# Attention of a decoder step on one Trainium2 core: four looped turns with pages loaded by half, against one written-out plan with 17 page places handed out in the order of use

## What is computed

```python
def diff_attention(q, k, v, q_pos, k_pos, rel_bias, lam, subln_g, lam_init):
    ...
    s = jnp.where(mask, s + bias, -jnp.inf)
    p = jax.nn.softmax(s, axis=-1)
    w = p[:, 0] - lam * p[:, 1]
    o = jnp.einsum('bhqk,bkhe->bqhe', w, v.astype(jnp.float32))
    o = o * lax.rsqrt(jnp.mean(o * o, axis=-1, keepdims=True) + SUBLN_EPS)
    ...
def stick_breaking_attention(q, k, v, q_pos, k_pos):
    ...
    log_rest = jnp.where(mask, jax.nn.log_sigmoid(-z), 0.0)
    suffix = lax.cumsum(log_rest, axis=3, reverse=True) - log_rest
    a = jnp.where(mask, jnp.exp(log_beta + suffix), 0.0)
    o = jnp.einsum('bhqk,bkhd->bqhd', a, v.astype(jnp.float32))
```

## Time and profile before

| | us |
|---|---|
| median of 3 runs | 1790.29 (1786.23 to 1792.81) |
| the profiled execution's own time | 1786.58 |
| its span, first to last instruction | 1784.7 |
| TensorE busy (matmuls) | 1381.3 (77%) |
| VectorE busy | 818.6 (46%) |
| ScalarE busy | 726.3 (41%) |
| DMA engines busy, mean share | 52% (q1 45.2%, q0 4.1%, q10 3.0%) |
| granted TensorE clock, mean | 0.890 |

### The profile page before, as it was taken

One profiled execution on the slowest core, in us unless ns is written; L12 is line 12 of the kernel. 1 busy time (PEld: TensorE's weight loads), 2 busy tenths in 40 slices (PEclk: granted clock), 3 DMA queues, 4 the chain that ended last, 5 costly groups with the idle time before them and its releaser, 6 DMA issues. The chain is left out here.

```text
span 1784.7 us, 30335 instructions
## 1 busy us (share of the span) xinstructions
PE 1381.3 (77%) x8924; PEld 1028.4 (58%) x8924; DVE 818.6 (46%) x1129; ACT 726.3 (41%) x1109; POOL 267.0 (15%) x200
## 2 busy tenths in 40 slices
PE   7999999967878787587878786688834888989930
PEld 4777778744545555354545453577623776777730
DVE  7021111125454545275757476322254555667635
ACT  5122221215454545353535354211104666677721
POOL 1000000000000000000000000000003455556644
PEclk9999999979898998798989998788856999999975
DMA  5333223146667666466666665432206799652248
GB/s 182 93 118 122 83 57 120 59 146 206 218 215 228 213 232 216 165 205 217 212 217 213 219 212 203 150 122 94 94 23 235 279 354 349 237 188 103 107 158 313
DMA packets 166779, 320.28 MB, mean 179 GB/s; under 512 B 20455, under 2 KB 59914, under 8 KB 162570
## 3 DMA queue, kind: packets, MB, share of 16 engines
q1 hardware_dynamic: 152666, 271.89, 45.2%
q0 software_dynamic: 7200, 26.22, 4.1%
q10 hardware_dynamic: 6800, 20.98, 3.0%
HBM read 313.33 MB, written 56.56 MB: 207 GB/s over the span
## 5 line engine op out<-in xcount | busy, mean ns | idle before, releaser
L1920 PE MATMUL gate_up_ps<-w_gate_up_split,slot_rows_T 128*128 128x512 f32 x768 | 196.3, 414 | 31.8 <-DVE slot_rows_T L1972 31.7
L1964 DVE TENSOR_TENSOR w_gate_up_split<-w_gate_up,w_gate_up_split 128x2048 fp32r<-128x2048 f32 x64 | 143.8, 2288 | 133.4 <-ACT w_gate_up_split L2018 133.4
L1888 POOL TENSOR_TENSOR w_down_split<-w_down,w_down_split 128x2048 fp32r<-128x2048 f32 x32 | 170.4, 5325 | 163.7 <-ACT w_down_split L2026 163.7
L874 PE MATMUL turns_and_scores_ps<-ident,pages 128*128 128x128 f32 (+1 forms) x1088 | 151.9, 286 | 53.1 <-DMA pages<-in_cache_s 31.4
L1920 PEld LDWEIGHTS gate_up_ps<-w_gate_up_split,slot_rows_T 128*128 128x128 f32 x768 | 150.5, 199 | 70.9 <-DVE slot_rows_T L1972 38.7
L255 PE MATMUL proj_ps<-w_in_hi,h_T_hi 128*128 128x512 f32 x432 | 174.4, 404 | 9.4 <-DVE w_in_lo L305 9.4
L874 PEld LDWEIGHTS turns_and_scores_ps<-ident,pages 128*128 128x128 f32 (+1 forms) x1088 | 125.0, 149 | 96.7 <-issue 95.8
L255 PE MATMUL proj_ps<-w_in_hi,h_T_lo 128*128 128x512 f32 x432 | 171.3, 396 | 0.0
L255 PE MATMUL proj_ps<-w_in_lo,h_T_hi 128*128 128x512 f32 x432 | 171.2, 396 | 0.0
L2018 ACT ACTIVATE w_gate_up_split<-w_gate_up 128x2048 fp32r x64 | 119.1, 1909 | 121.4 <-DMA w_gate_up<-in_w_up 86.6
L350 ACT ACTIVATE proj_rows<-proj_ps,sum_squares 128x512 f32<-128x512 f32 x54 | 37.1, 689 | 277.3 <-PE proj_ps L255 260.2
(11 more groups left out here) (220 smaller groups left out, 2150.5 us busy)
## 6 DMA issues: line engine op xcount, KB each, us to landing
pages<-in_cache_d SPq DMA_DIRECT2D x256, 256.0 KB, 3.1
pages<-in_cache_s SPq DMA_DIRECT2D x256, 256.0 KB, 3.1
w_gate_up<-in_w_gate SPq DMA_DIRECT2D x32, 1024.0 KB
w_gate_up<-in_w_up SPq DMA_DIRECT2D x32, 1024.0 KB
w_down<-in_w_down SPq DMA_DIRECT2D x32, 1024.0 KB
scratch_moe_out<-expert_out ACTq DMA_DIRECT2D x32, 512.0 KB
w_in_now<-in_w_in SPq DMA_DIRECT2D x48, 256.0 KB, 5.2
x_tiles<-in_x SPq DMA_DIRECT2D x9, 512.0 KB, 7.7
```

Of the source, the lines that this page charges most:

```text
L874: last = pe.transpose(kT_ps[:, KIND_BLOCKS * e + b, 0:n], page_rows[0:n, p, e, b, :], t.ident[0:n, 0:n])
L1888: pool.tensor_tensor(dn_split[:, u, 1, :, :], w_dn[:, bass.ds(at, 1), :, :].rearrange("p a k n -> p (a k) n"), dn_split[:, u, 0, :, :].bit ...
L1920: last = pe.matmul(gu_ps[:, u, :], xT[:, u, a, k, :], gu_split[:, u, b, k, :], start=(k == 0 and m == 0), stop=(k == KC - 1 and m == 2))
L1964: dve.tensor_tensor(gu_split[:, u, 1, at, :].rearrange("p k (c n) -> p k c n", c=2), raw[:, at, :, :], gu_split[:, u, 0, at, :].bitcast(F3 ...
```

## The change

The loops over turns go: the list of steps now covers all four turns, each engine walks it once, and every step carries its turn `it`. `prompt_steps` runs on from the last tile of a turn to the first of the next. Keys of turn it+1 are used between the values of turn it. Pages have 17 places (`PAGE_PLACES`) that keys and values take in the order of use: SP loads the first 17 uses, and after each use loads the use that is 17 further on. q, k, v, near (DIFF) and oT have two buffers each. Page scores take places in the ring (57 uses per turn in DIFF, 53 in STICK), and the sample output keeps a bank alone. The store of oT goes from ScalarE to SP. In DIFF the reciprocal of the sample sums goes from `weigh` to `rows`; in STICK the product of the sample weights is made in two parts, pages 0 to 7 first.

```diff
-SPANS = {DIFF: ((0.02, 0.45), (0.45, 0.53), (0.56, 1.0)), STICK: ((0.02, 0.45), (0.45, 0.53), (0.56, 1.0))}
+N_WEIGH = {DIFF: 2, STICK: 3}
+PAGE_PLACES = 17
+FIRST_KEYS, LAG, END_KEYS = 0.30, 0.02, 0.31
+WEIGH_AT, USE_AT, END_USE = 0.34, 0.42, 0.30
...
+    tiles = [(it, i) for it in range(TURNS) for i in range(PT)]
+    out = scores(0, 0) + scores(0, 1) + soft(0, 0, 0) + soft(0, 0, 1) + soft(0, 0, 2)
+    for n, (it, i) in enumerate(tiles):
+        one = tiles[n + 1] if n + 1 < len(tiles) else None
+        two = tiles[n + 2] if n + 2 < len(tiles) else None
+        out += soft(*one, 0) if one else []
...
+        if i == 1 and it:
+            out.append((("store", it - 1), 0))
...
+    for it in range(TURNS):
...
+        use = [(("turn", it, g), 1) for g in range(V_GROUPS)]
+        use += [(("apply", it, p), 2) for p in range(D_PAGES)] + [(("rows", it), 1), (("heads", it), 1)]
+        step = (TURNS - END_USE) / TURNS
+        begin = it * step
+        timed += spread_over(pages, 0 if it == 0 else begin - step + USE_AT + LAG, FIRST_KEYS if it == 0 else begin + END_KEYS)
+        timed += spread_over([(("weigh", it, n), 1) for n in range(N_WEIGH[kind])], begin + WEIGH_AT, begin + USE_AT - 0.02)
+        timed += spread_over(use, begin + USE_AT, begin + step + END_USE)
+    timed.sort(key=lambda x: x[0])
...
-        if name not in ("score", "page", "turn", "turn_out") and not (
+        if name not in ("score", "page", "page_scores", "turn", "turn_out") and not (
...
-        page_rows = sb("pages", [P, D_PAGES, PAIR, KIND_BLOCKS, P])
+        page_rows = sb("pages", [P, PAGE_PLACES, PAIR, KIND_BLOCKS, P])
...
+        page_uses = [step for step in plan if step[0] in ("page", "apply")]
+        use_no = {step: n for n, step in enumerate(page_uses)}
+        def page_here(engine, *step):
+            n = use_no[step]
+            engine.wait_ge(page_loaded[n % PAGE_PLACES], 32 * (n // PAGE_PLACES) + 32)
+            return page_rows[:, n % PAGE_PLACES, :, :, :]
...
-                    if half == 0:
-                        sp.wait_ge(applied.sem, applied.after(it, p - D_PAGES))
-                    else:
-                        sp.wait_ge(kT_done.sem, kT_done.after(it, p))
...
+                            at = (it * PAIR + e) * N_PAGES + p
+                            page = sp.value_load(t.pages[0:1, at:at + 1], min_val=0, max_val=t.n_pool - 1)
...
+                def load_next(*step):
+                    n = use_no[step] + PAGE_PLACES
+                    if n < len(page_uses):
+                        load_page(*page_uses[n])
+                def load_head(it):
+                    u, block = it % 2, it + TURNS * kind
+                    if it >= 2:
+                        sp.wait_ge(sc_done.sem, sc_done.after(it - 1, -1))
+                    sp.dma_start(qT[:, u, :], t.qT[:, block, 0:SEQ]).then_inc(qk_loaded[u], 16)
+                    sp.dma_start(kT[:, u, :], t.kT[:, block, 0:SEQ]).then_inc(qk_loaded[u], 16)
...
+                def page(it, p):
+                    sp.wait_ge(kT_done.sem, kT_done.after(it, p))
+                    own_wait(sp, t)
+                    load_next("page", it, p)
+                def apply(it, p):
+                    sp.wait_ge(applied.sem, applied.after(it, p))
+                    own_wait(sp, t)
+                    load_next("apply", it, p)
+                def score(it, i, g):
+                    if chunks[g][0:2] == (3, 0) and it + 1 < TURNS:
+                        load_head(it + 1)
+                def store(it):
...
+                    sp.dma_start(t.oT[:, it + TURNS * kind, 0:SEQ], oT[:, it % 2, :]).then_inc(oT_stored[it % 2], 16)
...
+                for n in range(PAGE_PLACES):
+                    if n == 2:
+                        load_head(0)
+                    load_page(*page_uses[n])
+                for name, *args in plan:
+                    if name in steps:
+                        steps[name](*args)
...
-                with pe.Fori(0, TURNS) as it:
-                    for name, *args in plan:
-                        if name in steps:
-                            steps[name](it, *args)
+                for name, *args in plan:
+                    if name in steps:
+                        steps[name](*args)
...
-                    elif n == 2:
-                        dve.wait_ge(sweighed.sem, sweighed.after(it, 0))
-                        dve.reciprocal(sstat[:, 2:3], sstat[:, 1:2]).then_inc(sinv.sem, 1)
...
+                        first = PER_TURN * PAGE
+                        keys = slice(0, first) if n == 1 else slice(first, KEYS)
+                        dve.tensor_tensor(sW[:, keys], sW[:, keys], s_left[:, keys.start + 1:keys.stop + 1], ALU.mult)\
+                           .then_inc(sweighed.sem, 1)
```

More of the change, by code:

```diff
@@ L529, in score_group_pages @@
     return range(2 * g, min(2 * g + 2, D_PAGES))
-def attention_plan(kind):
[L536 to L559, removed]
-        else:
[L561 to L579, removed]
-    timed = []
[L581 to L585, removed]
@@ new lines, in spread_over, with prompt_steps, scores, soft @@
+def spread_over(steps, begin, end):
+    of, done, out = sum(w for _, w in steps), 0, []
+    for step, w in steps:
+        out.append((begin + (end - begin) * done / of, step))
+        done += w
+    return out
+def prompt_steps(kind):
+    chunks = score_chunks(kind)
+    def scores(it, i):
+        return [(("score", it, i, g), SCORE_COST[kind]) for g, c in enumerate(chunks) if c[0] == i]
+    def soft(it, i, n):
+        return [(("soft", it, i, n), 2 + 2 * i)]
+    def turns(it, i):
+        return [(("out", it, i, n), 10) for n in range(len(turned_groups(kind, i)))]
+    def product(it, i):
+        return [(("out", it, i, len(turned_groups(kind, i))), 3 + 2 * i)]
+    tiles = [(it, i) for it in range(TURNS) for i in range(PT)]
+    after = dict(zip(tiles, tiles[1:]))
+    out = scores(0, 0) + scores(0, 1) + soft(0, 0, 0) + soft(0, 0, 1) + soft(0, 0, 2)
[3 more added lines that the diff above has]
+        out += soft(*one, 0) if one else []
+        if kind == DIFF:
+            out += soft(*one, 1) if one else []
+            out += scores(*two) if two else []
+            out += turns(it, i)
+            out += [(("turn_out", *tiles[n - 1]), 3)] if n else []
+        else:
+            out += turns(it, i)
+            out += soft(*one, 1) if one else []
+            out += scores(*two) if two else []
+        out += soft(*one, 2) if one else []
+        out += product(it, i)
+        if i == 1 and it:
+            out.append((("store", it - 1), 0))
+    if kind == DIFF:
+        out.append((("turn_out", *tiles[-1]), 3))
+    return out + [(("store", TURNS - 1), 0)]
@@ new lines, in attention_plan @@
+def attention_plan(kind):
+    prompt = prompt_steps(kind)
+    timed = []
+    for it in range(TURNS):
+        pages = []
+        for p in range(D_PAGES):
+            pages.append((("page", it, p), 2))
+            if p >= 2 and p % 2 == 0:
+                pages.append((("page_scores", it, p // 2 - 1), 1))
+        pages.append((("page_scores", it, S_GROUPS - 1), 1))
+        use = [(("turn", it, g), 1) for g in range(V_GROUPS)]
[6 more added lines that the diff above has]
+    timed.sort(key=lambda x: x[0])
+    total = sum(w for _, w in prompt) / TURNS
@@ L611, in ring_places @@
         total[place] += 2 if both else 1
-    return places, reads, total
+    return places, reads
 def attention(nc, t, kind):
@@ L772, in _ @@
+                def store(it):
+                    if kind == DIFF:
+                        kept(sp, "turn_out", it, PT - 1)
+                    else:
+                        sp.wait_ge(oT_kept.sem, oT_kept.after(it, PT - 1))
+                    sp.dma_start(t.oT[:, it + TURNS * kind, 0:SEQ], oT[:, it % 2, :]).then_inc(oT_stored[it % 2], 16)
+                steps = dict(score=score, page=page, apply=apply, store=store)
                 if kind == DIFF:
@@ L807, in _ @@
                 if kind == DIFF:
-                    with pool.Fori(0, TURNS) as it:
+                    for it in range(TURNS):
                         for i in range(PT):
@@ L1131, in score @@
                     _, k0, k1, kn = chunks[g]
-                    end, z = (i + 1) * P, ring[places["score", i, g]]
+                    end, z = (i + 1) * P, ring[places["score", it, i, g]]
                     if kind == DIFF:
```

301 lines of the change are left out of this document (138 added, 163 removed).

## The result

The changed kernel takes 1770.3 us (median of 4 runs, 1765.44 to 1776.92) against 1790.9 us: ratio 0.9887, 95% interval 0.9863 to 0.9912. It is faster by 20.6 us where 44 were forecast. Its profiled execution took 1765.44 us, 21.1 less than the 1786.58 of the one before. All of that is in attention.

| us | DIFF | STICK | DIFF, to last key transpose + rest |
|---|---|---|---|
| before | 356.1 | 355.8 | 312.9 + 43.1 |
| after | 347.8 | 342.3 | 290.4 + 57.5 |
| forecast | 336 | 336 | 281 + 55 |

A forecast was written before the change was run, and what follows sets the result against it. Attention was taken as SP's page-issue loop that TensorE follows: 278 + 55 + 3 = 336 us per block against 357, 42 us gained over both, median 1746 us; the 8 in 10 range was 1714 to 1778.

The forecast's parts named there:

- SP's queue: Page issues in attention: one stretch per block at 2.2 to 2.3 us per use, last key landed at 278 us.
- The tail: End of each attention block after the last key page: remaining prompt work and the last turn's values, 55 us.
- The coupling: Loss in each attention block from SP's and TensorE's chains being of equal length: 3 us.
- TensorE's turn: One turn of attention in the new order, by TensorE's work and remaining waits: 79 us in both kinds.
- The sum by TensorE: Attention block by TensorE: four turns of 79 us, 12 of waiting, 4 of start and end, 332 us.
- The reciprocal: In DIFF, VectorE's reciprocal no longer waits for the sample exponentials: 3 us off each turn.
- the two sums meet: Per attention block, SP's 333 us and TensorE's 332 us agree, so neither alone sets the end.
- Rival 1: In attention, other waits replace those for loads, TensorE's turn stays at 83 us: median 1772 us; chance 0.18.
- Rival 2: In attention, TensorE follows SP all the time and the end takes 45 us: median 1712 us; chance 0.12.
- Rival 3: In attention, start and end are paid but middle turns stay at 87.4 us: median 1808 us; chance 0.07.
- rival 4: SP's waits for TensorE before page loads keep places empty in attention: within 0.5% of no change; chance 0.07.
- Written-out code: Fetching four turns of attention instructions instead of one body: nothing, 1 us per turn as the upper end.

The follow-up runs named there:

- known_pages_after: The changed kernel with page numbers written in as constants, no number loads: 1717.7 us, ratio 0.9597 to the kernel before.
- no_bounds_after: The changed kernel without the range check behind each page number load: 1720.8 us, ratio 0.9624 to the kernel before.
- known_pages_before: The kernel before with page numbers counted from the loop's register, no number loads: 1769.9 us, ratio 0.9891 to the unedited kernel before.

## Why the prediction missed

**SP's queue.** That SP's queue would be one stretch of page issues at 2.2 to 2.3 us per use, without the gap of 4 us, held: 2.28 by 112 uses is 255.7 us, where 260 with the odd long issues were forecast. What lies between the uses was too small: the start 1.9 us before the first page (0), four head blocks 10.7 (7), two stores 4.6 (0.8), seven uses of new rows 8.0 (7.7). The 0.8 for the stores was named in the prediction but isn't in its sum. So the last key was issued at 281 us and landed at 284 in DIFF, for 278.

**The tail** after the last key is 57.5 and 59.1 us for 55.

**The coupling** of two chains of equal length was put at 3 us. In DIFF TensorE ends the last key's transposes at 290.4, 6.5 behind its landing; in STICK the whole part up to it is 283.2. The three make the block: 6 + 3.5 + 2.5 = 12 us over the forecast in DIFF, 342.3 - 336 = 6 in STICK, 18 of the 21 us by which the profiled execution (1765.4 for 1744.6) missed. The remaining 3 lie in the blocks before, which are 356 and not 357, and in what is outside.

**TensorE's turn.** The sum by TensorE, 332, was too long, not too short: with SP relieved the blocks are 326 and 311 (known_pages_after), 327 and 315 (no_bounds_after), in STICK a turn of some 74 us for the 79 of the sum. Two of its terms were too favourable, and the order gave TensorE more than the rest of them, so that in DIFF the errors nearly cancelled. The reciprocal, to which 3 us went, gives nothing by itself. And a DIFF turn of the kernel before without waits for loads was put at 82 us with TensorE's busy time unchanged. With the loads relieved it is 86 to 88 (known_pages_before): the idle time fell by 3 to 5 us, where the prediction took off 5.5, but the matmuls took 3 to 6 us more at the lower clock. The reading that attention was a loop of SP of some 87 us that TensorE follows was half the truth: SP's queue showed no pause, but TensorE's chain, at the clock that it then got, was as long.

**The failed step of the sum** is thus where "the two sums meet", with SP's as the bound, at 278 + 55 + 3 = 336 us for a block. The bound was right: SP's queue is full, and 59 us added to it make a block 58 us longer. Its small terms were put too low, the head blocks, stores and start between the page uses above all (17 us for 7), then the coupling and the tail; the blocks are 348 and 342. A gain of 21 us per block that is the difference of two sums of 357 and 336 falls to less than half when 12 us of small pieces are left out. The clock, which the forecast held fixed, wasn't among its terms at all.

**Rival 1** has the right time, 1772, with the wrong mechanism, so that its number is luck: it set TensorE's turn at 83 by waits for VectorE and the ring. Those waits fell (35.6 to 26.5 in DIFF, and from 22.6 to 14.9 in STICK before the sample weights, though those for the scans rose from 4.0 to 13.5), and TensorE's own turn came out at (326 - 16) / 4 = 78. **Rival 2** had the end take 45 us and TensorE behind SP without a loss; the end took 57 to 59. **Rival 3** and **rival 4** are out: SP didn't wait, and no middle part got longer.

**The start.** TensorE waited 13.4 us for the key pages at a stroke and 4.6 for q and k, 18 for the 12 forecast.

**Written-out code.** Queue 8's fetches doubled, 32 packets to 64. The fetches that the Trainium skill (Advanced Engine Details and Errata, section ISA Cache) let one expect came, and TensorE's waits show no line that they would explain. But the other instruction queue, q14, had 81 packets of 8 KB before and has 73 now. SP's queue has a pause of about 0.35 us behind every 128th of its instructions, every 23 us or so, 3.8 us in all from 389 to 655 us, with whatever instruction stands there, and a packet of q14 starts 1 to 2 us behind each. The looped kernel has the same pauses, four in each of its turns, and in its later turns, 470 to 736 us, this is the only line of an instruction queue:

```profile
q14 instruction: 16, 0.13, 0.1%
```

So SP fetched its code in every turn of the loop already, and "Four turns of instructions must be fetched where one body was" doesn't hold for it. That the pause is the fetch is argued from these times, not shown.

**The number load.** The Trainium skill's floor of 600 ns for a `tensor_load` (DMA: Bandwidth & Descriptors, Latency and other measured facts) isn't what this trace shows: a median of 270 ns for the load itself (262 to 622), and (2.81 - 2.28) 0.53 us for a whole load with its check, 0.26 of which is the check.

## What to carry over

When an issuing queue shows no pause, price everything in it, the range checks and the pieces between the regular uses too, and then remove its cost in an experiment before believing that it alone sets the time: here another chain was as long. A new order and a cheaper queue are worth little apart (20 and 14 us) and 70 together. And when loads are issued from a second queue, look at the landing of the page that is needed next: with both queues fast, later pages landed before it.

## What wasn't expected of the hardware

- The range check behind a register load, a register operation of 152 ns and an assert of 18, costs 0.26 us of the queue per number with what lies between, as much as the load (0.27). Leaving it out of the 256 numbers of each block was worth 50 us in the new order and 14 in the old.
- A GpSimd issue of a page takes 538 ns against SP's 333.
- SP's queue pauses for about 0.35 us behind every 128th instruction, in looped and in written-out code alike.
- The same 2420 matmuls of DIFF's block were busy for 269 us at a granted clock of 0.92 and for 282 at 0.86. TensorE's idle time doesn't order these clocks: 0.92 stands in blocks with 57 and 79 us of it, 0.86 in blocks with 63 and 71. What sets it wasn't settled.
